# A four-layer hybrid decoder trunk on one core: the first layer's sums of squares spread between its first products, and the query-key products of a gated-delta layer placed in the middle of a half tile

## The reference, cut to what matters

```python
def rms_norm(x, g, eps=1e-6):
    return x * rsqrt(mean(x * x, axis=-1) + eps) * g

for i in range(4):
    h = rms_norm(x, norm_g[i])
    y = mixer[i % 3](h)      # A, B, C, A
    x = x + y

def deltanet_mixer(h, ...):
    proj = h @ w_in                                  # 6160 columns
    qkv = silu(causal_dwconv(proj[:4096], conv_w))   # 8 heads: q, k of 128, v of 256
    q, k = l2_norm(q), l2_norm(k)
    # gated delta rule in chunks:
    L     = strict(k_beta @ k.T * decay)             # key-key products
    intra = causal(q @ k.T * decay)                  # query-key products
    ...                                              # triangular solve, state, output
    return (rms_norm(o, g) * silu(gate)) @ w_out
```

## Time and profile before

| what | value |
|---|---|
| median of three runs | 1758.52 us |
| the profiled execution's own time | 1758.74 us |
| its span, first to last instruction | 1756.9 us |
| instructions | 22619 |
| TensorE matmul busy | 1741.8 us, 99% |
| VectorE busy | 887.9 us, 51% |
| ScalarE busy | 826.3 us, 47% |
| GpSimd busy | 654.1 us, 37% |
| the three fp32r passes on the chain that ended last | 22% each |

### The profile page before, as it was taken

The page is one execution under the profiler, slowest core; times in us unless marked ns, Lnnn a source line. Parts: engine busy times, 40 slices in busy tenths (PEclk is TensorE's granted clock), DMA queues, the critical chain, the costliest instruction groups (busy, mean ns, idle before and its releaser), DMA issues.

```text
span 1756.9 us, 22619 instructions
## 1 busy us (share of the span) xinstructions
PE 1741.8 (99%) x8786; PEld 1418.8 (81%) x8786; DVE 887.9 (51%) x1329; ACT 826.3 (47%) x1191; POOL 654.1 (37%) x238
## 2 busy tenths in 40 slices
PE   8999999999999999999999999999999999999999
PEld 6688899888898666678888888888877888998887
DVE  6765964453133777745734433341287568435500
ACT  5575343785233776744422222222266734348720
POOL 1333420344434655444244444444324234114442
PEclk9999999999999999999999999999999999999999
DMA  4223210222222111122222222222222232012222
GB/s 177 89 80 97 73 43 8 95 96 96 96 96 73 49 49 49 49 72 96 86 106 95 95 95 95 95 95 96 84 96 72 73 118 64 13 49 96 96 96 72
DMA packets 48776, 143.70 MB, mean 82 GB/s; under 512 B 28080, under 2 KB 30256, under 8 KB 32816
## 3 DMA queue, kind: packets, MB, share of 16 engines
q1 hardware_dynamic: 48688, 142.50, 23.9%
HBM read 137.25 MB, written 5.24 MB: 81 GB/s over the span
## 4 chain that ended last, share of the span: by engine, by line
PE 88%; DVE 6%; ACT 4%; issue 1%; DMA 0%; POOL 0%; SPq 0%; ACTq 0%; DVEq 0%
PE ps L1662 22%; PE ps L1664 22%; PE ps L1663 22%; PE ps L1928 3%; DVE acc L1154 2%; PE ps L1989 2%; PE ps L1955 2%; PE ps L2118 1%; PE ps L1975 1%; PE ps L1939 1%; PE ps L1984 1%; PE ps L2164 1%; DVE acc L1157 1%; PE ps L2062 1%; PE ps L2064 1%
## 5 line engine op out<-in xcount | busy, mean ns | idle before, releaser
L467 POOL TENSOR_TENSOR w_lo<-w_raw,w_hi 128x2048 fp32r<-128x2048 f32 x105 | 496.6, 4730 | 805.2 <-ACT w_hi L598 802.1
L1662 PE MATMUL ps<-h_hi,w_hi 128*128 128x512 f32 x1488 | 594.1, 399 | 4.2 <-DVE h_lo L1027 2.1
L1664 PE MATMUL ps<-h_hi,w_lo 128*128 128x512 f32 x1488 | 580.4, 390 | 0.0
L1663 PE MATMUL ps<-h_lo,w_hi 128*128 128x512 f32 x1488 | 579.5, 389 | 0.0
L1662 PEld LDWEIGHTS ps<-h_hi,w_hi 128*128 128x128 f32 x1488 | 279.4, 188 | 83.1 <-issue 21.1
L1664 PEld LDWEIGHTS ps<-h_hi,w_lo 128*128 128x128 f32 x1488 | 279.2, 188 | 59.8
L1663 PEld LDWEIGHTS ps<-h_lo,w_hi 128*128 128x128 f32 x1488 | 279.6, 188 | 55.9 <-issue 1.4
L598 ACT ACTIVATE w_hi<-w_raw 128x2048 fp32r<-128x2048 f32 (+1 forms) x126 | 238.7, 1895 | 129.4 <-PE ps L1664 123.8
L1662 PE MATMUL ps<-y_hi,w_hi 128*128 128x512 f32 x448 | 174.3, 389 | 0.0
L1663 PE MATMUL ps<-y_lo,w_hi 128*128 128x512 f32 x448 | 174.3, 389 | 0.0
L1664 PE MATMUL ps<-y_hi,w_lo 128*128 128x512 f32 x448 | 174.3, 389 | 0.0
(11 more groups left out here) (211 smaller groups left out, 2332.2 us busy)
## 6 DMA issues: line engine op xcount, KB each, us to landing
w_raw<-w_tiles SPq DMA_DIRECT2D x124, 1024.0 KB, 4.9
x<-x_t SPq DMA_DIRECT2D x4, 512.0 KB, 7.0
out_t<-x SPq DMA_DIRECT2D x8, 256.0 KB, 5.7
w_raw<-w_tiles SPq DMA_DIRECT2D x2, 512.0 KB, 5.0
scr_u<-lt SPq DMA_DIRECT2D x8, 128.0 KB, 2.7
u_blk<-scr_u SPq DMA_DIRECT2D x2, 512.0 KB, 3.3
scr_t<-v_t SPq DMA_DIRECT2D x2, 512.0 KB, 2.6
scr_v<-v_blk SPq DMA_DIRECT2D x2, 512.0 KB, 3.3
```

The source lines that it names most:

```text
L467: pool.tensor_tensor(w_lo[:, slot, :], w_raw[:, slot, :], w_hi[:, slot, :].bitcast(F32), ALU.subtract).then_inc(lo_done, 1)
L1662: pe.matmul(out_, w_h, m_h, start=start, stop=False)
L1663: pe.matmul(out_, w_h, m_l, start=False, stop=False)
L1664: return pe.matmul(out_, w_l, m_h, start=False, stop=stop)
```

## The change

Two edits on TensorE's program. The first layer's sums of squares stand behind blocks 1, 3 and 5 (two of them there) in place of blocks 4, 5, 6 and 7; the last two stay behind block 7. And `qk(n)`, which stood behind half n + 12, ahead of `kk` and `spreads`, now stands in the middle of half n + 13, between its blocks 3 and 4. The key-square sum in the middle of half 9 stays where it is; the gate halves pass a 0, by which nothing is inserted.

```diff
@@ first_tiles
-                if l == 0 and k >= 4:
-                    sum_first((0, 2, 4, 5)[k - 4])
+                if l == 0:
+                    for m in {1: (0,), 3: (2,), 5: (4, 5)}.get(k, ()):
+                        sum_first(m)
@@ in_half
-            def in_half(j, c, between=None):
+            def in_half(j, c, between):
                 if c == 0:
                     ready(t0 + j)
                 for k in range(KD):
-                    if k == KD // 2 and between is not None:
-                        k_sums(between)
+                    if k == KD // 2:
+                        if between == HEADS + 1:
+                            k_sums(HEADS - 1)
+                        if 0 <= between - PHASE1 - 3 < UNITS:
+                            qk(between - PHASE1 - 3)
                     mm = in_block(t0 + j, c, k)
                 mm.then_inc(proj_done, 1)
@@ the loop over halves
-                    in_half(j, c, HEADS - 1 if x_ == HEADS + 1 else None)
+                    in_half(j, c, x_)
...
                     u = x_ - PHASE1
-                    if 0 <= u - 2 < UNITS:
-                        qk(u - 2)
                     if 0 <= u - 1 < UNITS:
                         kk(u - 1)
                     if 0 <= u < UNITS:
@@ the gate halves
-                in_half(17 + h, 0)
+                in_half(17 + h, 0, 0)
...
-                in_half(17 + h, 1)
+                in_half(17 + h, 1, 0)
```

## The result

The changed kernel takes 1768.53 us in the median of six runs (1766.13 to 1771.03), beside 1758.74 for the kernel before (six runs, 1758.38 to 1759.18). The ratio is 1.0054, 95% interval 1.0044 to 1.0065: slower by 9.8 us, where 3.6 had been forecast and the range ended at 1766.0. One execution of experiment 6 took 5301 us; it counts as slow and enters no interval. The profiled execution took 1768.67 us, with a span 10.0 us longer than before.

What follows compares the result with a forecast made beforehand. TensorE, busy 99% of the 1756.9 us span, was taken as the bound. Moved sums +2.0 and query-key products +1.6 gave +3.6 us on the median 1758.52: 1762.1 us, range 1760.0 to 1766.0.

Steps and rivals of the forecast that it cites:

- the sum of 3.6: Whole kernel: +2.0 us for the first sum's wait at the start, +1.6 for unit 0's query-key product in both layers.
- One small term: After half 12: kk(1) could start at about 109.10 in place of 109.19, so 0.09 us came off the product's 0.89.
- the clock falls in the new gap: Rival, start: 4.5 us idleness drops TensorE to 1.2 GHz, costing 1.5 to 3.0 us more, sum 5.1 to 6.6; chance 0.26.
- the present gaps of 1.1 us: Start, old order: idle gaps of 1.06 and 1.05 us; two blocks at either side of each kept the higher clock.
- a sign to look for: Both layers: a wait of about 2.6 us on `lt` before kk(1), in place of the one on the SiLU.
- The bounds for the middle: Query-key products in the middle of halves: extra price taken as 0.00, bounds 0 and 16 x 0.29 = 4.6 us.
- The faster rival: Start and both layers: all gaps filled, -1.7 and -3.8, together -5.5 us, 1753.0 us; chance of both 0.04.
- both releasers: Landing of constants `cb` at the start, and `lt`, late by line 1222 behind GpSimd's split; neither touched by the diff.

Runs made afterwards that it cites:

- experiment 6: Query-key edit alone in the kernel before, plus one fp32 product nobody reads ahead of the key-key product's wait for `lt` in each layer: 1761.01 us, ratio 1.0010.
- experiment 3: Query-key edit alone in the kernel before, but unit 0's product left at its old boundary and units 1 to 7 moved: 1759.07 us beside 1759.0, ratio 1.0003.
- experiment 10: Changed kernel with the first sum waiting only for the table of ones and VectorE's small instruction one half earlier: 1753.71 us beside 1758.74 for the kernel before.
- experiment 5: Changed kernel with five filler products ahead of the first sum and none in the layers: 1764.42 us beside 1759.11 for the kernel before, ratio 1.0032.
- experiment 1: Only the first layer's sums moved in the kernel before, query-key products as before: 1763.06 us beside 1759.0, ratio 1.0021.
- experiment 7: Sums moved alone in the kernel before, the first sum waiting only for the table of ones on its own semaphore: 1757.35 us beside 1758.74, ratio 0.9993.
- experiment 8: Query-key edit alone in the kernel before, with VectorE's 128x32 product issued one half earlier: 1754.92 us, ratio 0.9979.
- experiments 1 to 4: Sums moved alone, 1763.06 us; query-key edit alone, 1764.06; that edit without unit 0, 1759.07; changed kernel with fillers in its start and layer gaps, 1762.54.
- experiments 8 and 9: VectorE's 128x32 product one half earlier, with the query-key edit alone (1754.92 us) and in the otherwise unchanged kernel before (1758.85 us beside 1758.74).

## Why the prediction was wrong

**The signs and the waits were right.** The first sum waited until 16.1 for the constants (forecast 16.08). The key-key product waited 2.6 us for `lt` in both layers. The seven moved products of a layer were free, and the one at unit 0 cost what it no longer hid. With TensorE kept busy in the gaps, the sum of 3.6 measured 3.5. One small term was wrong: kk(1) was to start 0.09 sooner without the product in front of it, but it starts 0.14 behind the end of `lt` in the changed kernel (113.99 beside 113.85) as it did before (0.15), so nothing was gained there.

**The step that failed is the price of the idleness on the clock.** The forecast had TensorE at its full clock behind every gap, and so put this term at nothing. At the start it stood among the rivals, "the clock falls in the new gap", with a chance of 0.26 and 1.5 to 3.0 us; it measured 4.80 - 2.0 = 2.8. The forecast leaned on the argument that the present gaps of 1.1 us had kept the higher level, which tells nothing of one of 4.5. By the rule of the Trainium skill ("TensorE: Matmul & The Clock Gate", section "Why this matters for your kernels"), a long idle gap between bursts of matmuls sends the engine back to its lower clock. The traces bear this out only in part: behind the wait at the start the clock was low, but it had fallen before that wait began, at about 11.5; and in the layers it fell behind 2.61 to 2.66 us of idleness, less than the gaps that the page warns of.

**The larger omission was the other place.** The prediction named the gap of 2.6 us ahead of kk(1), listed it even as a sign to look for, and priced it at what it shifts alone. It asked what the longer idleness does to the clock only at the start. The gap grew from 1.6 to 2.6 us, and that was enough: 7.25 - 4.80 = 2.45 and 9.85 - 7.32 = 2.53 us a layer in place of 0.8. Of these 0.89 are the query-key product, and 1.6 each are the clock's. Had the same question been put to all three gaps, with the prices now measured, the rival would have been 2.0 + 2.8 + 2 x 2.5 = 9.8 us. Its top was 6.6, and so the range ended too low.

**The bounds for the middle** (0 to 4.6 us) were needlessly wide on the upper side; going by line 1844 at 163.21 and not by the narrow key-square sum was right (experiment 3).

**The faster rival** gave -5.5 if both releasers were out of the way. Taking them out (experiment 10) gave -5.0. So the idea of both edits was sound, and each lacked one neighbouring edit. I had both mends in hand as the two releasers, and they were not part of the change.

## What to carry to other kernels

When a wait is moved or removed on an engine in program order, read what the next instruction behind it waits for, and when that is satisfied: here each edit uncovered a wait that had been satisfied just in time, about 0.15 us ahead, in both places. A gap on TensorE that grows has two prices, the shift and the passes at half speed behind it; ask for both at every gap, and not only at the longest; where the wait can't be removed, a product that nobody reads may hold the clock.

## What the runs showed of the hardware

**In the layers TensorE's clock fell behind gaps of 2.6 us, and not behind gaps of 1.7.** Behind 1.70 and 1.67 us of idleness (experiment 6) and 1.62 the key-key or query-key group ran at 2.4 GHz. Behind gaps of 2.61 to 2.66 the clock fell to 1.2 GHz in five of the six places of the three profiled executions that had them, and not in the sixth (2.62, experiment 5). The fall comes up to 1 us behind the end of the gap: in layer 3 of the changed kernel the key-key group still took 0.97 us, and the spreads behind it were the first at half speed. So the same gap cost 0 or 1.6 us, a likely part of the 4.9 us over which the changed kernel's runs scatter.

**The clock fell while TensorE worked, in three executions.** In the changed kernel's profiled execution the last two passes ahead of the new gap, at 11.29 and 11.56, take 0.47 and 0.63 us in place of 0.40: the granted clock falls at about 11.5, before that gap begins. What stands ahead of them, in its timeline, is this:

```profile
2.32 5.18 PE L2236 MATMUL ps<-rows 128*128 128x512 f32 x9
10.26 0.50 PE L1662 MATMUL ps<-h_hi,w_hi 128*128 128x512 f32 x1 [2.76 <-DVE w_lo L1035]
```

The warm-up ended at 7.50 here and at 8.91 in the trace before, since the clock rose sooner within it (weight loads 0.43 us apart from 4.77 on; in the earlier trace rows only from 7.45). The same five products were over 1.4 us sooner, and the gap up to the first real one was 2.76 us in place of 0.98. With the start filled (experiment 5, whose gap there was 2.74) TensorE's timeline and the stretches read:

```profile
11.97 5.75 PE L1697 MATMUL ps<-rows 128*128 128x512 f32 x10
17.56 1.02 PE L1703 MATMUL ps<-sq,cf 128*128 128x512 f32 x2
```

```profile
0.00:11.40 11.40, 7.35 (x15) 3.54 (x16) 3.24 (x4) 6.20 (x9) 1.62 (x6) 0.99 0.83 283
11.40:16.00 4.60, 4.60 (x9) 2.13 (x9) 4.49 (x7) 4.30 (x7) 0.06 (x1) 0.66 1.03 431
16.00:24.00 8.00, 8.00 (x27) 4.58 (x26) 5.00 (x6) 2.12 (x2) 0.99 (x2) 1.00 0.37 123
```

The clock fell there too, at about 11.2, and was back before 16 with the fillers running; at half speed these outlasted the wait, and the first sum began at 17.56 in place of 16.1. In the changed kernel the wait for the constants followed at once, and the clock stayed low to 21.7. So in these executions the wait at the start did not begin the low spell; it prolonged it. Whether it would begin one by itself, behind a warm-up that ends late, no profiled execution shows. But all ten runs of edit one alone lost 3.0 us or more, where the wait is worth 2.0, while the times of the kernel before hint at an early fall in a few runs only (below); so it is likely.

The earlier gap is the likely cause of the early fall, and its length doesn't decide alone. Ahead of the first real product, gaps of 2.76, 2.74 and 2.43 us (experiment 1) were followed by a fall 1.1 to 1.4 us behind the gap's end; gaps of 2.42 (experiment 7), 2.14 (experiment 8) and 2.12 (experiment 6) by none.

**An early fall may also explain a scatter of the kernel before.** Of the thirty runs beside experiments 1 to 4, five took 1760.0 to 1760.4 us with a mean granted clock of 0.998, and the other twenty-five 1758.1 to 1759.5 with 0.999 or 1.000. I take them for executions in which the warm-up ended early and the clock fell at 11; no profile shows one of them, so this is a guess.

**A small instruction of VectorE that started beside a weight split of GpSimd ended only with it.** The 128x32 product of line 1222, whose two inputs `der` and `tok` both lie in SBUF, took 3.41 and 3.39 us in the kernel before and 3.38 in the changed one beside a weight split of GpSimd, and 0.18 away from it (experiments 8 and 9). It ended 0.05 behind the split in the earlier trace rows. The products `k_beta` (0.69 us at 104.42 in the kernel before) and `lt` (0.68 at 104.84 in experiment 8), which read one input from PSUM, took no longer beside such a split.
